# A two-model transformer kernel on one core: order of the work at block one's seams

## Chip, cores and metric

One NeuronCore of a Trainium2 chip. The metric is the device time of one launch in microseconds (us); the median of several runs counts. Engines are named as in the profile: PE is TensorE (PEld its weight loads), DVE is VectorE, ACT is ScalarE, POOL is GpSimd, SP is SyncE, which here issues every DMA. An "L" number is a line of the kernel before, unless the text says that it is one of the changed kernel.

## What is computed

256 tokens of width 1024 pass through two layers of a first block and then two layers of a second one. The change touches the first block, and the places where one layer follows another. Cut to that:

```python
for l in range(2):                                   # first block
    h = rms_norm(x, attn_norm_g[l])
    proj = h @ w_in[l]          # latents, GQA q/k/v, pool input, gate logits
    ...                         # three branches, each gated, summed in merged
    x = x + merged @ w_out[l]
    hf = rms_norm(x, ffn_norm_g[l])
    u = depthwise_conv(hf @ ffn_w_up[l], ...)        # 3 taps along the tokens
    u_gate, u_val = u[..., :2816], u[..., 2816:]
    x = x + (silu(u_gate) * u_val) @ ffn_w_down[l]
for i in range(2):                                   # second block
    h = x @ w_in_2[i]           # no norm ahead of it
    ...                         # two attentions, layer norm, 32 experts, layer norm
```

## The kernel before

**Parts.** Everything is float32, and the dense products are made of three passes over rounded parts. A weight chunk of up to 128 x 2048 lands by DMA in one of three `raw` slots (1 MB each). ACT rounds it to `w_hi` (L253, "hi" of the chunk), DVE subtracts to get `w_lo` (L258, "lo"), and `mm3` (L286) runs hi x hi, lo x hi and hi x lo on PE (L288 to L290). Activations are split in the same way: `one_hT_hi` by ACT (L373) and `one_hT_lo` by DVE (L381), each out of the PSUM tile that PE's transposes filled. `Stream` counts chunks: `hi_to` and `lo_to` split all chunks up to a name, `parts` makes PE wait for the lo part, and a raw slot may be loaded again once the lo part of the chunk in it is made.

**Lots.** PSUM is used as four lots of two banks (2 x 512 floats a partition). A hand-written list, `order` in `block_one`, says which tile uses which lot in which turn; `claim` waits until the last user of the lot is drained.

**Order.** Each engine has a program written out by hand (`sync`, `tensor`, `scalar`, `vector` of `block_one` and `block_two`); an engine runs its own in order and waits on semaphores. The 256 tokens are two tiles, t0 and t1, of 128.

**Start of a layer of block one.** DVE makes statistics of x (`first_stats`), ACT the root (`root_act_of`, L805), DVE scales (`rms_scale`, L837, into `one_tmp`), PE transposes eight 128 x 128 pieces (`transpose_tile`, L848), ACT and DVE split the result (`xTt0`, `xTt1`), and PE multiplies with `lat0` and `lat1` (`first_part`, 128x416), then `gkv` (128x256), `gq`, `uq`, `ukv`, `pool0` and `pool1`. In layer 0, tables for block two are loaded (`load_tables`, after `pool1` in SP's program), DVE makes angles of them (`rotation_angles`, L1918 on) and ACT their sines (`rotation_sines`, L1905).

**From attention to the FFN.** `out_part` adds the product with `w_out` in lots `wot0` and `wot1`; DVE adds it to x (`add_out`, `add_halves`), the second norm follows in the same way (`fTt0`, `fTt1`), and PE starts the FFN when both tiles are split.

**FFN.** Eleven steps of 256 hidden columns (`ffn_pe`). A step's up product `H` is 2 banks (G for the gate, U for the value) x 2 x 8 x 3 = 96 matmuls of 128x256: the weights are the stationary side and all 256 tokens the moving one. A profile row names the moving operand first, so `lot<-one_hT_hi,w_hi 128x256` is such a matmul. ACT and DVE do the convolution's taps, silu, product and its hi and lo parts (`h_lo`, L755), while PE does the next step's H; then comes the down product `D` (24 matmuls of 128x512), and DVE adds its tiles `Y` to x (L1744; the last ones by halves, `add_last`, L1449, inside the next layer's program).

**Between the layers of block two.** PE runs 36 transposes of the identity (`E.warm(pe, SEAM_TURNS)`, L2282) whose results nobody reads, then the transposes of x and `ik`, whose matmuls are 128x72.

Of the kernel before, what the change touches and what calls it, by code (L numbers as in the profile page):

```python
# [23 lines left out]
ALU = mybir.AluOpType  # L24
# [52 lines left out]
SEAM_TURNS = 36  # L77
# [560 lines left out]
def ffn_ends(steps):  # L638
    return {f"U{e}": f"H{e}" for e in range(steps)} | {f"D{e}": f"Y{e}t1" for e in range(steps)}
# [49 lines left out]
def ffn_pe(K, L, ST, pe, steps, xT, h):  # L689
# [12 lines left out]
    def down(e, i=None):  # L702
        pe.wait_ge(K.sig["h_lo"], K.sig.at("h_lo", later(e + 1, i, 2)))
        for t in range(T):
            lot = L.claim(pe, f"Y{e}t{t}", i, 2)
            w = [v[:, 0:CHUNK].rearrange("p (k c) -> p k c", k=T) for v in ST.parts(pe, f"D{e}", i)]
            for n in range(2):
                for k in range(T):
                    last = mm3(pe, K.ps[lot][:, n, :], [v[:, e % 2, k, t * P:(t + 1) * P] for v in h],
                               [v[:, k, n * 512:(n + 1) * 512] for v in w], k == 0, k == T - 1)  # L710
                if i is None and e == steps - 1 and n == 0:
                    last.then_inc(K.sig["last_half"], 1)
            last.then_inc(L.filled(f"Y{e}t{t}"), 1)

    hidden(0)

    def step(e, i):
        hidden(e + 1, i)
        down(e, i)

    ffn_walk(pe, steps, step)
    down(steps - 1)


def ffn_act(K, L, ST, act, steps, first, second, wait_full, h_hi, tail):
# [21 lines left out]
    tail()  # L747
    high(e, None)


def ffn_dve(K, L, ST, dve, steps, first, second, add, h, enter, leave, tail):
# [28 lines left out]
    e = steps - 1  # L780
    tail()
    for t in range(T):
        L.wait_filled(dve, f"Y{e - 1}t{t}")
        L.wait_before(dve, f"Y{e - 1}t{t}")
        add(e - 1, None, t).then_inc(L.drained(f"Y{e - 1}t{t}"), 1)
        if t == 0:
            low(e, None)
# [158 lines left out]
def block_one(K, M, layer, before=None, tables=None):  # L946
    nc, A, sig, st = K.nc, K.A, K.sig, K.stat
    names = ONE_CHUNKS + ffn_chunks(FF_STEPS)
    order = [("xTt0", 2), ("xTt1", 3), ("lat", 0), ("gkv", 2), ("gq", 3), ("cT", 1), ("q0", 2), ("q1", 0), ("kv0", 1),
# [12 lines left out]
    stage.L, stage.ST, stage.sig = L, ST, sig  # L962
# [54 lines left out]
    def sync(sp):  # L1017

        if before is None:
            for t in range(T):  # L1020
                sp.dma_start(K.x[:, t, :], A["x"][0][t * P:(t + 1) * P, :]).then_inc(sig[f"x_in{t}"], 16)
# [4 lines left out]
        for name in ONE_CHUNKS:  # L1026
# [24 lines left out]
    def tensor(pe):  # L1051
# [218 lines left out]
        for t in range(T):  # L1270
            L.wait_drained(pe, f"fTt{t}")
        ffn_pe(K, L, ST, pe, FF_STEPS, hT, (M.h_hi, M.h_lo))

    def scalar(act):
# [39 lines left out]
        ST.hi_to(act, "ukv")  # L1314
        take("gq", M.lat[:, :, C_GQ:C_GK], lambda ps: ps[:, :, :])
# [7 lines left out]
        if tables:  # L1323
            rotation_sines(sig, tables, act)
# [92 lines left out]
        def last_step():  # L1417
# [4 lines left out]
            for b in range(2):  # L1422
# [14 lines left out]
                lambda e, i: act.wait_ge(sig["h_full"], sig.at("h_full", later(e + 1, i, 2))), M.h_hi, last_step)  # L1437

    def add_last(dve, link, t, c):
# [16 lines left out]
    def vector(dve, link):  # L1456
# [8 lines left out]
        def first_stats(t):  # L1465

            if before is None:
                dve.wait_ge(sig[f"x_in{t}"], 16)
            for c in range(2):
                if before:  # L1470
                    before.add_last(dve, link, t, c)
                last = stats_of(K, dve, t, c)
            link(last)
# [2088 lines left out]
```

## Time and profile before

| | us |
|---|---|
| median of 3 runs (lowest, highest) | 1821.15 (1818.53, 1832.74) |
| the profiled execution: device time | 1821.87 |
| the profiled execution: span from first to last instruction | 1820.0 |
| PE busy in the span | 1632.6 (90%) |
| DVE busy | 1095.7 (60%) |
| ACT busy | 749.0 (41%) |
| mean granted TensorE clock, share of 2.4 GHz | 0.958 |

A timeline row gives start, length, engine, line, operation, output and inputs, how many instructions were merged, and in brackets how long the engine had been idle and what ended it. The granted clock of a stretch (PEclk) is 1.00 at 2.4 GHz and 0.50 at 1.2 GHz.

### The profile page before, as it was taken

How to read it: one execution, taken by the hardware profiler on the slowest of the kernel's cores; microseconds unless marked ns; L12 is line 12 of the kernel's file. 1: busy time of each engine (PE TensorE's matmuls, PEld its weight loads, DVE VectorE, ACT ScalarE, POOL GpSimd, SP SyncE). 2: the span in 40 equal slices, each digit the busy share in tenths (PEclk: the TensorE clock that was granted, in tenths of full speed). 3: DMA queues.
4: the chain of work that ended last, by engine and by line, in shares of the span. 5: the costliest groups of instructions: out<-in, count | busy, mean ns of one | idle time of the engine just before them, and what ended most of it. 6: DMA issues, size and time to landing. Idle time of an engine off the chain costs nothing.

```text
span 1820.0 us, 25937 instructions
## 1 busy us (share of the span) xinstructions
PE 1632.6 (90%) x10562; PEld 1288.5 (71%) x10562; DVE 1095.7 (60%) x1550; ACT 749.0 (41%) x976; POOL 0.2 (0%) x4
## 2 busy tenths in 40 slices
PE   6999989998999989999999898968789998897776
PEld 5777779997887779998887676434468776753433
DVE  5776768778786857878477673222265966512124
ACT  3556545554546635554456541101034655311111
POOL 0000000000000000000000000000000000000000
PEclk9999999998999999999999999889999999899988
DMA  6552536554552445554544398999956437799996
GB/s 205 182 185 93 174 119 206 184 196 140 184 190 101 145 145 198 172 184 146 193 166 135 122 413 331 412 418 412 409 162 208 140 115 286 313 414 417 412 416 244
DMA packets 174271, 422.54 MB, mean 232 GB/s; under 512 B 15984, under 2 KB 68568, under 8 KB 157528
## 3 DMA queue, kind: packets, MB, share of 16 engines
q1 hardware_dynamic: 174168, 421.07, 63.0%
q8 instruction: 76, 1.25, 0.3%
q14 instruction: 27, 0.22, 0.0%
HBM read 419.99 MB, written 1.05 MB: 231 GB/s over the span
## 4 chain that ended last, share of the span: by engine, by line
PE 60%; DVE 15%; DMA 15%; issue 4%; ACT 3%; SPq 3%; DVEq 0%; ACTq 0%
PE lot L288 15%; PE lot L290 14%; PE lot L289 14%; DVE w_lo L258 5%; PE lot L2218 4%; DMA raw<-w_exp_up 3%; SPq L2115 3%; DMA e_hi<-w_exp_down 3%; PE lot L2292 2%; ACT w_hi L253 2%; PE lot L2188 2%; DMA e_hi<-w_exp_up 1%; DMA raw<-w_out 1%; DMA two_e_sqT<-w_exp_up 1%; DMA e_lo<-w_exp_up 1%
## 5 line engine op out<-in xcount | busy, mean ns | idle before, releaser
L258 DVE TENSOR_TENSOR w_lo<-raw,w_hi 128x2048 fp32r<-128x2048 f32 (+4 forms) x196 | 436.1, 2230 | 127.4 <-ACT w_hi L253 126.7
L253 ACT ACTIVATE w_hi<-raw 128x2048 fp32r<-128x2048 f32 (+4 forms) x196 | 365.2, 1867 | 144.2 <-PE lot L290 129.6
L288 PE MATMUL lot<-one_hT_hi,w_hi 128*128 128x256 f32 x704 | 200.9, 285 | 5.1 <-DVE one_hT_lo L381 5.1
L289 PE MATMUL lot<-one_hT_lo,w_hi 128*128 128x256 f32 x704 | 200.7, 285 | 0.0
L290 PE MATMUL lot<-one_hT_hi,w_lo 128*128 128x256 f32 x704 | 200.6, 285 | 0.0
L288 PE MATMUL lot<-w_hi,two_hT_hi 128*128 128x512 f32 (+1 forms) x448 | 180.6, 403 | 9.7 <-DVE two_hT_lo L381 4.2
L290 PE MATMUL lot<-w_hi,two_hT_lo 128*128 128x512 f32 (+1 forms) x448 | 175.6, 392 | 0.0
L289 PE MATMUL lot<-w_lo,two_hT_hi 128*128 128x512 f32 (+1 forms) x448 | 175.5, 392 | 0.0
L288 PE MATMUL lot<-w_hi,one_hT_hi 128*128 128x512 f32 (+2 forms) x384 | 151.5, 395 | 15.6 <-DVE w_lo L258 6.7
L290 PE MATMUL lot<-w_hi,one_hT_lo 128*128 128x512 f32 (+2 forms) x384 | 147.2, 383 | 0.0
L289 PE MATMUL lot<-w_lo,one_hT_hi 128*128 128x512 f32 (+2 forms) x384 | 147.0, 383 | 0.0
L288 PEld LDWEIGHTS lot<-one_hT_hi,w_hi 128*128 128x128 f32 x704 | 136.7, 194 | 6.4 <-issue 5.7
L289 PEld LDWEIGHTS lot<-one_hT_lo,w_hi 128*128 128x128 f32 x704 | 136.7, 194 | 0.7
L290 PEld LDWEIGHTS lot<-one_hT_hi,w_lo 128*128 128x128 f32 x704 | 136.6, 194 | 0.0
L288 PEld LDWEIGHTS lot<-w_hi,two_hT_hi 128*128 128x128 f32 x448 | 87.9, 196 | 30.9 <-issue 7.4
L1734 DVE SCALAR_TENSOR_TENSOR one_conv<-lot,one_cols,one_conv 128x255 f32<-128x255 f32 x160 | 66.2, 476 | 58.2 <-ACT one_conv L1408 55.7
L290 PEld LDWEIGHTS lot<-w_hi,two_hT_lo 128*128 128x128 f32 x448 | 87.5, 195 | 17.7
L289 PEld LDWEIGHTS lot<-w_lo,two_hT_hi 128*128 128x128 f32 x448 | 87.8, 196 | 15.5
L288 PEld LDWEIGHTS lot<-w_hi,one_hT_hi 128*128 128x128 f32 x384 | 73.7, 192 | 34.0 <-issue 14.3
L2338 DVE COPY two_xw<-lot 128x512 f32<-128x512 f32 x16 | 11.1, 692 | 132.7 <-PE lot L2188 132.7
L2218 PE MATMUL lot<-raw,two_xw 128*32 128x256 f32 x448 | 82.1, 454 | 9.1 <-DMA e_hi<-w_exp_up 6.4
L2392 DVE TENSOR_TENSOR two_y_lo<-lot,two_y_hi 128x1024 fp32r<-128x1024 f32 x14 | 17.1, 1224 | 114.1 <-ACT two_y_hi L2359 114.1
(435 smaller groups left out, 3250.3 us busy)
## 6 DMA issues: line engine op xcount, KB each, us to landing
raw<-w_in SPq DMA_DIRECT2D x78, 1024.0 KB, 4.9
raw<-ffn_w_up SPq DMA_DIRECT2D x44, 1024.0 KB, 5.1
raw<-ffn_w_down SPq DMA_DIRECT2D x22, 1024.0 KB, 4.9
raw<-w_out SPq DMA_DIRECT2D x16, 1024.0 KB, 6.4
raw<-w_exp_gate SPq DMA_DIRECT2D x14, 1024.0 KB, 18.4
raw<-w_exp_up SPq DMA_DIRECT2D x14, 1024.0 KB, 20.6
two_e_gates<-w_exp_up SPq DMA_DIRECT2D x12, 1024.0 KB, 19.7
e_lo<-w_exp_up SPq DMA_DIRECT2D x10, 1024.0 KB, 22.1
```

Of the source, the lines that this page charges most:

```text
L253: act.activation(K.hi[:, r, 0:n], self.raw(name)[:, 0:n], ACT.Copy).then_inc(K.sig["hi_ready"], 1)
L258: dve.tensor_tensor(K.lo[:, r, 0:n], self.raw(name)[:, 0:n], K.hi[:, r, 0:n].bitcast(F32), ALU.subtract).then_inc(K.sig["lo_ready"], 1)
L288: pe.matmul(out, a[0], b[0], start=start, stop=False)
L289: pe.matmul(out, a[0], b[1], start=False, stop=False)
L290: return pe.matmul(out, a[1], b[0], start=False, stop=stop)
L1734: last = dve.scalar_tensor_tensor(dst, src, w, dst, ALU.mult, ALU.add)
L2115: sp.dma_start(dst.rearrange("p (k c) -> p k c", k=self.parts[name[0]]), self.source(name[0], expert)).then_inc(self.landed(name), 16)
L2188: last = pe.matmul(K.ps[1][:, lot - 2, kk * QE * CAP:(kk + 1) * QE * CAP], M.xg[:, t, k, :], M.rows01[:, t, :], start=t == 0, stop=t == T - 1)
L2218: last = pe.matmul(K.ps[0][j * CAP:(j + 1) * CAP, lot, half * D_E:(half + 1) * D_E], M.xw[:, k, rows], w[j][:, k, :], start=k == 0, stop=k ...
L2292: last = pe.matmul(K.ps[1][:, lot - 2, :], M.nT[:, k, t * P:(t + 1) * P], w[:, k % 4, :], start=k == 0, stop=k == KD - 1)
L2338: dve.tensor_copy(dst, src).then_inc(self.L.drained(f"X{q}.{j}"), 1)
L2392: dve.tensor_tensor(self.M.y_lo[:, s, :], flat(self.K.ps[2][:, :, :]), self.M.y_hi[:, s, :].bitcast(F32), ALU.subtract).then_inc(self.L.dr ...
```

## The change

1. **First FFN step by token tile.** The last quarter of `w_out` (`out_part(1, 1, 1)`) now runs ahead of the transposes of `fTt0`. The up product of step 0 is cut by token tile: G and U for t0, then for t1, 48 matmuls of 128x128 in each of four pieces, 192 in place of 96. The transposes of `fTt1` stand behind the first piece. DVE splits `G0` earlier, adds both halves before it makes the lo part of t0, and the statistics of the second half come behind that.
2. **Last two down products in one lot.** Steps 9 and 10 of the down product accumulate in the same PSUM lots; DVE's two additions of step 9 to x (128x1024 each) are gone. The H and Y lots of the last step and most lots at the layer's start are others.
3. **Order at a layer's start.** ACT takes the root of t0 and the hi part of t0 before it splits more weights; DVE makes the lo part of `lat0` and of t0 before the second half of t1's statistics. At the end of a layer ACT splits the next layer's first chunk before the hidden part's hi.
4. **Loads in layer 0.** x's second tile is loaded behind `lat0`; the tables behind `gq0`, not behind `pool1`; ACT makes the sines before it takes `gq` out of PSUM.
5. **Between the layers of block two** the 36 transposes of the identity are gone.

```diff
 def ffn_lots(steps):
     order = [("H0", 0)]
-    for e in range(1, steps):
+    for e in range(1, steps - 1):
         order += [(f"H{e}", e % 2), (f"Y{e - 1}t0", 2), (f"Y{e - 1}t1", 3)]
-    return order + [(f"Y{steps - 1}t0", (steps - 1) % 2), (f"Y{steps - 1}t1", steps % 2)]
+    e = steps - 1
+    return order + [(f"H{e}", e % 2), (f"Y{e}t0", 2), (f"Y{e}t1", 3)]
...
+    def down_two():
+        e = steps - 1
+        pe.wait_ge(K.sig["h_lo"], K.sig.at("h_lo", e))
+        for t in range(T):
+            lot = L.claim(pe, f"Y{e}t{t}")
+            for n in range(2):
+                last = part(e - 1, lot, t, n, stop=False)
+        ST.done(last, f"D{e - 1}")
+        pe.wait_ge(K.sig["h_lo"], K.sig.at("h_lo", e + 1))
+        for t in range(T):
+            lot = L.use[f"Y{e}t{t}"][0]
+            part(e, lot, t, 0, start=False).then_inc(K.sig["last_half"], 1)
+            part(e, lot, t, 1, start=False).then_inc(L.filled(f"Y{e}t{t}"), 1)
...
     tail()
+    if after:
+        after.ST.hi_to(act, after.first)
     high(e, None)
...
-    order = [("xTt0", 2), ("xTt1", 3), ("lat", 0), ("gkv", 2), ("gq", 3), ("cT", 1), ("q0", 2), ("q1", 0), ("kv0", 1),
+    order = [("xTt0", 1), ("xTt1", 0), ("lat", 2), ("gkv", 1), ("gq", 0), ("cT", 3), ("q0", 2), ("q1", 1), ("kv0", 0),
...
+            if before is None and name == "lat0":
+                sp.dma_start(K.x[:, 1, :], A["x"][0][P:S, :]).then_inc(sig["x_in1"], 16)
-            if tables and name == "pool1":
+            if tables and name == "gq0":
+                load_tables(nc, A, sig, tables, sp)
                 sp.dma_start(K.rope[:, :, :], A["c_rope"]).then_inc(sig["rope_in"], 16)
-                load_tables(nc, A, sig, tables, sp)
...
+        out_part(1, 1, 1).then_inc(L.filled("wot1"), 1)
         transpose_tile(K, L, pe, M.tmp, "fTt0", 0, sig, "n2_normed")
-        out_part(1, 1, 1).then_inc(L.filled("wot1"), 1)
+        def first_hidden(bank, t):
+            name = "GU"[bank] + "0"
+            w = [v[:, 0:CHUNK].rearrange("p (k c) -> p k c", k=KD) for v in ST.parts(pe, name)]
+            for f in range(2):
+                for k in range(KD):
+                    last = mm3(pe, K.ps[L.use["H0"][0]][:, bank, f * S + t * P:f * S + (t + 1) * P],
+                               [v[:, k, f * P:(f + 1) * P] for v in w], [v[:, k, t * P:(t + 1) * P] for v in hT],
+                               k == 0, k == KD - 1)
...
+        L.claim(pe, "H0")
+        L.wait_drained(pe, "fTt0")
+        first_hidden(0, 0)
         transpose_tile(K, L, pe, M.tmp, "fTt1", 1, sig, "n2_normed")
-        for t in range(T):
-            L.wait_drained(pe, f"fTt{t}")
+        first_hidden(1, 0)
+        L.wait_drained(pe, "fTt1")
+        first_hidden(0, 1)
+        first_hidden(1, 1)
...
-        ST.hi_to(act, "lat0")
-        root_act_of(K, act, "n1", 0)
+        if before:
+            ST.hi_to(act, "lat1")
+        root_act_of(K, act, "n1", 0)
+        ST.hi_to(act, "lat0")
+        tile_hi(0)
         ST.hi_to(act, "lat1")
         root_act_of(K, act, "n1", 1)
-        tile_hi(0)
         tile_hi(1)
...
-        first_stats(0)
+        first_stats(0, 0)
+        first_stats(0, 1)
         rms_var(K, dve, link, "n1", 0)
         rms_scale(K, dve, link, "n1", 0, M.tmp, M.gain)
-        first_stats(1)
+        ST.lo_to(dve, "lat0")
+        first_stats(1, 0)
+        tile_lo(0)
+        first_stats(1, 1)
         rms_var(K, dve, link, "n1", 1)
-        ST.lo_to(dve, "lat0")
-        tile_lo(0)
...
-        add_halves(1)
+        ST.lo_to(dve, "G0")
+        add_half(1, 0)
+        stats_of(K, dve, 1, 0)
+        add_half(1, 1)
+        low_tile(0)
+        link(stats_of(K, dve, 1, 1))
         rms_var(K, dve, link, "n2", 1)
         rms_scale(K, dve, link, "n2", 1, M.tmp, M.gain)
-        ST.lo_to(dve, "G0")
+        ST.lo_to(dve, "U0")
         low_tile(1)
...
-        if before:
-            E.warm(pe, SEAM_TURNS)
-        else:
+        if ahead:
             ahead.L.wait_drained(pe, f"Y{FF_STEPS - 1}t0")
```

How the rows of three places change. On PE, from attention to the FFN, the kernel before has behind the last quarter of `w_out` the transposes of `fTt1` (L848) and then step 0 with all 256 tokens:

```order
L290 MATMUL lot<-w_hi,one_hT_lo 128x512
L848 MATMUL lot<-ident,one_tmp 128x128 [waits n2_normed,drained1]
L848 MATMUL lot<-ident,one_tmp 128x128 x3
L848 MATMUL lot<-ident,one_tmp 128x128 [waits n2_normed]
L848 MATMUL lot<-ident,one_tmp 128x128 x3
L288 MATMUL lot<-one_hT_hi,w_hi 128x256 [waits drained0,lo_ready,drained1,drained2]
L289 MATMUL lot<-one_hT_lo,w_hi 128x256
L290 MATMUL lot<-one_hT_hi,w_lo 128x256
```

The changed kernel has there the transposes of `fTt0` (its line L861) and then step 0 for tile t0 alone:

```order
L289 MATMUL lot<-w_hi,one_hT_lo 128x512
L861 MATMUL lot<-ident,one_tmp 128x128 [waits n2_normed,drained2]
L861 MATMUL lot<-ident,one_tmp 128x128 x3
L861 MATMUL lot<-ident,one_tmp 128x128 [waits n2_normed]
L861 MATMUL lot<-ident,one_tmp 128x128 x3
L287 MATMUL lot<-one_hT_hi,w_hi 128x128 [waits lo_ready,drained2,drained0]
L288 MATMUL lot<-one_hT_lo,w_hi 128x128
L289 MATMUL lot<-one_hT_hi,w_lo 128x128
```

The wait for tile t1 (drained1) has moved behind the first two pieces, and the moving side has become 128 wide.

On DVE, from the end of the FFN of layer 0 to the start of layer 1, before (L1744 adds a tile of step 9, L1449 is `add_last`, L258 the lo part of `lat0`):

```order
L1768 TENSOR_TENSOR one_conv<-one_conv 128x512 [waits silu,drained0]
L1744 TENSOR_TENSOR x<-x,lot 128x1024 [waits drained2,filled2]
L755 TENSOR_TENSOR one_h_lo<-one_conv,one_h_hi 128x512 [waits h_hi]
L1744 TENSOR_TENSOR x<-x,lot 128x1024 [waits drained3,filled3]
L258 TENSOR_TENSOR w_lo<-raw,w_hi 128x1664 [waits hi_ready]
L1449 TENSOR_TENSOR x<-x,lot 128x512 [waits drained2,last_half]
```

And in the changed kernel:

```order
L1805 TENSOR_TENSOR one_conv<-one_conv 128x512 [waits silu,drained0]
L774 TENSOR_TENSOR one_h_lo<-one_conv,one_h_hi 128x512 [waits h_hi]
L257 TENSOR_TENSOR w_lo<-raw,w_hi 128x1664 [waits hi_ready]
L1484 TENSOR_TENSOR x<-x,lot 128x512 [waits drained2,last_half]
L831 BN_STATS stat<-x 128x6 [waits dve_chain]
```

The two additions between the hidden part and the last halves are gone.

On ACT, at the very start, before (L253 is the hi part of `lat0`, then `lat1`; L805 the roots; L373 the hi parts of t0 and t1):

```order
L253 ACTIVATE w_hi<-raw 128x1664 [waits landed1]
L805 ACTIVATE stat<-stat 128x1 [waits n1_var]
L253 ACTIVATE w_hi<-raw 128x1664 [waits landed2]
L805 ACTIVATE stat<-stat 128x1 [waits n1_var]
L373 ACTIVATE one_hT_hi<-lot 128x8x128 [waits filled2]
L373 ACTIVATE one_hT_hi<-lot 128x8x128 [waits filled3]
```

And in the changed kernel:

```order
L818 ACTIVATE stat<-stat 128x1 [waits n1_var]
L252 ACTIVATE w_hi<-raw 128x1664 [waits landed1]
L372 ACTIVATE one_hT_hi<-lot 128x8x128 [waits filled1]
L252 ACTIVATE w_hi<-raw 128x1664 [waits landed2]
L818 ACTIVATE stat<-stat 128x1 [waits n1_var]
L372 ACTIVATE one_hT_hi<-lot 128x8x128 [waits filled0]
```

The first root no longer stands behind the landing of `lat0`, and the hi part of t0 no longer behind `lat1`.

## Rows read from the trace of the kernel before

**Rows 1.** The page's part 1: busy time, share of the span and instructions of PE.

```profile
PE 1632.6 (90%) x10562; PEld 1288.5 (71%) x10562; DVE 1095.7 (60%) x1550; ACT 749.0 (41%) x976; POOL 0.2 (0%) x4
```

**Rows 2.** Timeline of the first 20 us; last row: DMA issues, median us to landing.

```profile
11.59 1.59 ACT L253 ACTIVATE w_hi<-raw 128x1664 fp32r<-128x1664 f32 x1 [5.40 <-DMA raw<-w_in]
...
14.40 1.94 PE L848 MATMUL lot<-ident,one_tmp 128*128 128x128 f32 x8 [14.40 <-DVE one_tmp L837]
...
16.71 1.88 DVE L258 TENSOR_TENSOR w_lo<-raw,w_hi 128x1664 fp32r<-128x1664 f32 x1
...
19.78 0.71 PE L288 MATMUL lot<-w_hi,one_hT_hi 128*128 128x416 f32 x1 [3.44 <-DVE one_hT_lo L381]
...
one_gain<-attn_norm_g SPq DMA_DIRECT2D x1, 512.0 KB, 7.3
```

**Rows 3.** Timeline of layer 0 around the tables of block two, 50 to 101 us.

```profile
50.42 1.90 ACT L253 ACTIVATE w_hi<-raw 128x2048 fp32r<-128x2048 f32 x1
...
55.72 0.29 DVE L1918 CAST two_tri_r<-two_tri 128x256 fp32r<-128x256 f32 x1 [8.69 <-DMA two_slots<-c_slots]
...
58.07 2.28 DVE L258 TENSOR_TENSOR w_lo<-raw,w_hi 128x2048 fp32r<-128x2048 f32 x1
58.13 1.28 ACT L1905 ACT_TABLE_LOAD   x1
...
60.50 0.47 PE L288 MATMUL lot<-w_hi,one_hT_hi 128*128 128x512 f32 x1 [4.11 <-DVE w_lo L258]
...
100.74 0.47 PE L288 MATMUL lot<-w_hi,one_hT_hi 128*128 128x512 f32 x1 [0.96 <-DVE w_lo L258]
```

**Rows 4.** Timeline of layer 0 from attention to the first FFN steps.

```profile
240.94 1.29 PE L848 MATMUL lot<-ident,one_tmp 128*128 128x128 f32 x8 [3.50 <-DVE one_tmp L837]
...
242.26 1.02 ACT L373 ACTIVATE one_hT_hi<-lot 128x1024 fp32r<-128x1024 f32 x1 [2.45 <-PE lot L848]
243.57 1.22 DVE L381 TENSOR_TENSOR one_hT_lo<-lot,one_hT_hi 128x1024 fp32r<-128x1024 f32 x1
...
244.89 0.55 PE L288 MATMUL lot<-one_hT_hi,w_hi 128*128 128x256 f32 x1 [2.66 <-DVE one_hT_lo L381]
...
271.39 0.50 PE L288 MATMUL lot<-w_hi,one_h_hi 128*128 128x512 f32 x1 [1.52 <-DVE one_h_lo L755]
```

**Rows 5.** Stretches, PE alone: length, busy time (matmuls), granted clock, DMA.

```profile
244.89:248.81 3.92, 3.92 (x18) 0.50 0.87 285
250.00:260.00 10.00, 10.00 (x86) 1.00 0.57 205
859.80:864.20 4.40, 4.40 (x23) 0.50 0.83 183
864.20:870.00 5.80, 5.80 (x17) 0.50 1.04 387
```

**Rows 6.** PE at the start of block two: the two pieces of 128x72.

```profile
859.41 0.27 PE L288 MATMUL lot<-w_hi,two_hT_hi 128*128 128x72 f32 x1 [1.51 <-DVE two_hT_lo L381]
...
860.34 0.41 PE L288 MATMUL lot<-w_hi,two_hT_hi 128*128 128x72 f32 x1
...
863.97 0.41 PE L290 MATMUL lot<-w_hi,two_hT_lo 128*128 128x72 f32 x1
...
870.31 0.28 PE L288 MATMUL lot<-w_hi,two_hT_hi 128*128 128x72 f32 x1
...
872.21 0.28 PE L290 MATMUL lot<-w_hi,two_hT_lo 128*128 128x72 f32 x1
```

**Rows 7.** PE from the FFN of layer 0 to layer 1.

```profile
438.55 1.23 PE L848 MATMUL lot<-ident,one_tmp 128*128 128x128 f32 x8 [2.74 <-DVE one_tmp L837]
...
444.90 0.69 PE L288 MATMUL lot<-w_hi,one_hT_hi 128*128 128x416 f32 x1 [5.12 <-issue]
```

**Rows 8.** PE between the layers of block two.

```profile
1332.32 3.22 PE L2282 MATMUL lot<-ident 128*128 128x128 f32 x28 [2.18 <-issue]
...
1339.05 0.27 PE L288 MATMUL lot<-w_hi,two_hT_hi 128*128 128x72 f32 x1 [2.64 <-DVE two_hT_lo L381]
```

More of the change, by code:

```diff
@@ L705, in down, with part, ffn_act @@
             lot = L.claim(pe, f"Y{e}t{t}", i, 2)
-            w = [v[:, 0:CHUNK].rearrange("p (k c) -> p k c", k=T) for v in ST.parts(pe, f"D{e}", i)]
             for n in range(2):
[L708 to L712, printed above, removed]
-            last.then_inc(L.filled(f"Y{e}t{t}"), 1)
-    hidden(0)
+                last = part(e, lot, t, n, i)
+            last.then_inc(L.filled(f"Y{e}t{t}"), 1)
+    def part(e, lot, t, n, i=None, start=True, stop=True):
+        w = [v[:, 0:CHUNK].rearrange("p (k c) -> p k c", k=T) for v in ST.parts(pe, f"D{e}", i)]
+        for k in range(T):
+            last = mm3(pe, K.ps[lot][:, n, :], [v[:, e % 2, k, t * P:(t + 1) * P] for v in h],
+                       [v[:, k, n * 512:(n + 1) * 512] for v in w], start and k == 0, stop and k == T - 1)
+        return last
+    def down_two():
[11 more added lines that the diff above has]
+            part(e, lot, t, 1, start=False).then_inc(L.filled(f"Y{e}t{t}"), 1)
     def step(e, i):
         hidden(e + 1, i)
-        down(e, i)
+        if i is None and e == steps - 2:
+            down_two()
+        else:
+            down(e, i)
     ffn_walk(pe, steps, step)
-    down(steps - 1)
-def ffn_act(K, L, ST, act, steps, first, second, wait_full, h_hi, tail):
+def ffn_act(K, L, ST, act, steps, first, second, wait_full, h_hi, tail, after):
     def high(e, i):
@@ L779, in ffn_dve @@
     ffn_walk(dve, steps, step, enter, leave)
-    e = steps - 1
     tail()
-    for t in range(T):
[L783 to L787, printed above, removed]
+    low(steps - 1, None)
 ONE_CHUNKS = ["lat0", "lat1", "gkv", "gq0", "gq1", "uq", "ukv", "pool0", "pool1", "g4a", "g4b", "window",
@@ L961, in block_one @@
     stage = Layer()
-    stage.L, stage.ST, stage.sig = L, ST, sig
+    stage.L, stage.ST, stage.sig, stage.first, stage.after = L, ST, sig, "lat0", None
     K.h = M.conv[:, 1, :, :]
@@ L1019, in sync @@
         if before is None:
-            for t in range(T):
-                sp.dma_start(K.x[:, t, :], A["x"][0][t * P:(t + 1) * P, :]).then_inc(sig[f"x_in{t}"], 16)
+            sp.dma_start(K.x[:, 0, :], A["x"][0][0:P, :]).then_inc(sig["x_in0"], 16)
             sp.dma_start(K.ident[:, :], A["c_ident"]).then_inc(sig["ident_in"], 16)
@@ L1314, in scalar @@
         ST.hi_to(act, "ukv")
+        if tables:
+            rotation_sines(sig, tables, act)
         take("gq", M.lat[:, :, C_GQ:C_GK], lambda ps: ps[:, :, :])
@@ L1322, in scalar @@
             take(f"kv{t}", M.kv[:, t, :])
-        if tables:
-            rotation_sines(sig, tables, act)
         ST.hi_to(act, "g4a")
@@ L1436, in scalar @@
         ffn_act(K, L, ST, act, FF_STEPS, middle_tap, silu,
-                lambda e, i: act.wait_ge(sig["h_full"], sig.at("h_full", later(e + 1, i, 2))), M.h_hi, last_step)
+                lambda e, i: act.wait_ge(sig["h_full"], sig.at("h_full", later(e + 1, i, 2))), M.h_hi, last_step, stage.after)
     def add_last(dve, link, t, c):
@@ L1463, in mul, with first_stats @@
             return dve.tensor_tensor(out, a, b, ALU.mult)
-        def first_stats(t):
-            if before is None:
+        def first_stats(t, c):
+            if before:
+                before.add_last(dve, link, t, c)
+            elif c == 0:
                 dve.wait_ge(sig[f"x_in{t}"], 16)
-            for c in range(2):
-                if before:
-                    before.add_last(dve, link, t, c)
-                last = stats_of(K, dve, t, c)
-            link(last)
+            last = stats_of(K, dve, t, c)
+            if c:
+                link(last)
         def tile_lo(t):
@@ L2504, in block_two @@
     stage = Layer()
-    stage.L, stage.ST, stage.after = L, ST, None
+    stage.L, stage.ST, stage.first, stage.after = L, ST, "ik", None
     x_sig, x_normed = (before.sig, "n2_normed") if before else (None, None)
@@ L2654, in first_part @@
                     last.then_inc(L.filled(name), 1)
-        if before:
-            E.warm(pe, SEAM_TURNS)
-        else:
+        if ahead:
             ahead.L.wait_drained(pe, f"Y{FF_STEPS - 1}t0")
@@ L3509, in build @@
         two1 = block_two(K.layer(ONE_COUNTS, ONE_COUNTS, TWO_COUNTS), two, 1, before=two0, out=out)
-        two0.after = two1
+        one0.after, one1.after, two0.after = one1, two0, two1
         with nc.Block() as block:
```

38 lines of the change are left out of this document (18 added, 20 removed).

## The prediction

> **What bounds the kernel now.** I read the page's part 1 first: PE is busy 90% of the span [rows 1], so the time is PE's work plus the stretches in which PE waits. Then the list of who waited for whom, for PE alone, and the timeline at each wait that the change touches. The reader is to see three things. At the start PE's first transposes come at 14.40 and its first product at 19.78; ACT stood behind the landing of `lat0` until 11.59 [rows 2]. At 60.50 PE waits 4.11 for a lo part that DVE makes late, because DVE had waited 8.69 for block two's tables [rows 3]. From attention to the FFN PE waits 3.50 and 2.66 [rows 4], and between the layers 2.74 and 5.12 [rows 7]. Last I read the granted clock of stretches and the pace of narrow matmuls [rows 5, 6], since the change makes 192 of them in each layer. There the sign is decided. All sums stand against the profiled execution: span 1820.0, device time 1821.87, which is 0.7 above the median of 1821.15; I carry the difference over to the median.
>
> **Start and tables (layer 0).** With the root first, DVE scales t0 as soon as the gain is there (issued at about 2.1, 7.3 to landing [rows 2]), so PE's transposes are done before `lat0` is split. From its landing the chain is hi 1.59, lo 1.88 [rows 2], half a tile's statistics (an estimate of 0.6, half of the 1.22 that DVE takes for a tile [rows 4]), lo of t0 1.22, handovers 0.2: 5.5. With `lat0` landing at 11.59 as before PE starts at 17.1; with x's 0.5 MB no longer ahead of it, it lands up to 1.35 earlier (0.52 MB at the 387 GB/s of [rows 5]) and PE starts at 15.8. So 2.7 to 4.0 are won; I take 4, since x1 is really moved behind `lat0`. The tables then are issued behind `gq0` and have landed long before DVE asks. ACT's hi part of `pool0` ended at 52.32 [rows 3]; it now ends at 52.3 - 4 + 1.7 (sine table load 1.28 and two short instructions, now ahead of it) = 50.0, and DVE's lo part starts there instead of at 58.07. DVE is busy without a gap from there until PE waits for it again at 100.74 [rows 3], so the whole stage moves by 8.1, and no more: PE alone could gain 4 + 4.1 + what the low clock behind that wait costs. Nothing gained if something else holds `pool0`: -4. Term: **-8.1** (-4 to -9).
>
> **FFN of layer 0 to layer 1.** Two additions to x are gone from DVE, and the lo part of t0 no longer waits for all of t1's statistics. PE's products end at 438.55 - 2.74 = 435.81 [rows 7]. The last half of t0 is added and scaled some 2 earlier, transposes at 436.4, hi and lo (1.02, 1.22 [rows 4]) behind them, DVE free for the lo part at 438.9: PE's product starts at 440.1, not at 444.90. What is late next is the lo part of `lat1`, made behind the scaling of t1: PE waits some 1 for it, of which 0.6 is a loss. The 48 matmuls of steps 9 and 10 stay 48, and the chunk split early on ACT fits where ACT idled. Term: **-4.2** (-1 to -5.5). From block one to block two PE is held by its own last product and a bare hi and lo chain: 0.
>
> **First FFN step by token tile (twice).** Before, PE's work ahead of the FFN ends at 240.94 - 3.50 = 237.44, then come wait, transposes, wait, and step 0 starts at 244.89 [rows 4]. After, the same work ends with the transposes of t0, and only their hi and lo (1.02 + 1.22, handovers 0.4) is bare: start at 240.1, 4.8 earlier. Against this stands the price of width. No row has a 128-wide product of rounded parts. From above: 256 wide takes 10.00/86 = 0.116 at 2.4 GHz and 3.92/18 = 0.218 at 1.2 GHz [rows 5]. From below: 72 wide takes (872.21 - 870.31)/17 = 0.112 and (863.97 - 860.34)/17 = 0.2135 [rows 6]. Narrowing to 72 saved 4% and nothing: something that doesn't shrink with the width, as loading the weights, sets the pace. So a 128-wide one costs 0.112 to 0.116, and 0.2135 to 0.218 at the lower clock; 96 become 192 at nearly the same price. At 2.4 GHz: 48 x 0.112 = 5.4, transposes 1.0, 144 x 0.112 = 16.1, so H0 is full at 262.6. Before it was full at 269.87 (= 271.39 - 1.52) less 96 x 0.117 = 258.6. That is +4.0, carried on, because the wait of 1.52 for the hidden part hangs on H0's end.
>
> The clock is the larger part. At the start of block two PE had the same pattern: wide matmuls, transposes, a wait of 1.51, narrow matmuls. The clock fell to 1.2 GHz within half a us of the first narrow one and stayed there through all the rest of them and 5.8 of wide ones [rows 5, 6]; elsewhere wide matmuls alone had it back after 3.92 [rows 5]. Here the wait is longer (2.3 to 2.7) and what follows is narrow again, now for more than 20 us. I expect the clock to fall about 1 us into the piece in four of five cases (how the wait lies in time decides), and to stay down until step 1's 256-wide ones have run for 4 to 6. Then: 0.9 at the high clock (8 matmuls), 184 x 0.2135 = 39.3, transposes 2.0: H0 full at 282.3. Step 1 takes 96 x 0.117 = 11.2 plus 2.5 for the low clock: 296.0, and by then the hidden part is ready, so no wait. Against 271.39: +24.6 a layer. Term for both layers: **+49.2** (+8 if the clock holds in both).
>
> The Trainium skill (TensorE: Matmul & The Clock Gate, Part 1) says that sustained matmuls release the throttle, and shows it on a stream of 128-wide ones. By that rule the clock would be back within the first quarter of the step and the total come to about 1824; rows 5 and 6 speak against it, as PE was busy without a gap there and the clock did not come back.
>
> **Between the layers of block two.** The 28 last identity transposes end at 1335.54 and hold back the real ones [rows 8]. Without them these start 2 earlier, the product about 0.9 earlier, since DVE is then the later one. But PE is idle where it was busy, the clock falls sooner and the 24 matmuls of 128x72 cost 24 x (0.2135 - 0.112) = 2.4 more, and a little behind them. Term: **+2** (-1 to +4).
>
> **Sum.** -8.1 - 4.2 + 0 + 49.2 + 2 = +38.9: 1821.87 becomes 1860.8, and the median 1821.15 becomes **1860**. The likeliest case has its own range of 1852 to 1867.
>
> **Rivals.**
> (a) *The low clock strikes in one layer only.* One wait lies so that the clock holds, and a step at the high clock keeps it. For it: the clock held across 1.52 at 271.39 [rows 4]. Then -8.1 - 4.2 + 2 + 24.6 + 4.0 = +18.3: 1839.
> (b) *The clock holds or comes back during the step, in both layers: not slower.* Its place is the four narrow pieces, its price 4.0 a layer, or 6 to 7 if it falls and returns after some 5 us. -8.1 - 4.2 + 2 + 8.0 = -2.3, up to +3: 1819 to 1824. It decides if 128-wide matmuls count as work for the clock where 72-wide ones didn't; between 72 and 256 no row tells. Against it: rows 5 and 6.
> (c) *The narrow matmuls are cheap.* If cost goes with width, 128 wide takes 0.058, the 192 take 11.2, the token split wins 6.3 a layer, and the clock has no reason to stay down: -8.1 - 4.2 + 2 - 12.6 = -22.9: 1798. Against it: 0.112 for 72 wide [rows 6]. The Trainium skill (same page, Back-to-back issue gap) gives 81 ns for a stream of 128-wide matmuls with their weight loads; by that the total would be about 1807, and the same rows contradict it for these operands.
> (d) *The change doesn't do what it says* at the start, because the gain or the first chunk lands later than I think: PE starts at 19 as before and the first term is -4. That only adds 4 to each case.
>
> **How the numbers follow.** Likeliest case 0.52, (a) 0.22, (b) 0.18, (c) 0.08. The range leaves out (c) and a little at the top: 1820 to 1867. Faster or slower by over 1% (18 us; about what a measurement of this kernel can tell from no change): faster only in (c), 0.06; slower in the likeliest case and in half of (a), 0.64; the rest, 0.30, within 1%.
>
> **What would show it.** Right: step 0's 192 matmuls take some 40 us with a granted clock of 0.50 over most of them, and spacings near 0.21; the page's mean clock falls below 0.958 by some 0.02. DVE waits under 1 for the tables, PE's first product comes at 16 to 17, and PE's wait at 60 is gone. Layer 1's first product comes 4 to 5 sooner behind the last down product. Wrong: narrow products spaced by 0.112 at a clock of 1.00 (then b), by 0.06 to 0.08 (then c), or a first product still near 19 (then d).

## The result, and the profile after

The changed kernel takes **1838.08 us** (median of 20 runs, 1823.22 to 1853.58) where the kernel before, beside it, took 1825.42 (20 runs, 1818.53 to 1834.82). The medians are 12.7 apart, a ratio of 1.0069. The ratio computed beside the runs is 1.0043, 95% interval 1.0025 to 1.0061; it leaves out the four runs at 1853 as disturbed, although here they are a state of the kernel's own, as shown below. The forecast was 1860, 38.9 more than the kernel before: the sign was right, the size three times too large.

The 20 times are three heaps: 5 runs from 1823.2 to 1824.8, 11 from 1835.4 to 1839.9, 4 from 1852.5 to 1853.6. The mean granted clock goes with them: 0.956 to 0.959, 0.944 to 0.950, 0.938 to 0.941. The profiled execution is one of the top heap: span 1851.7, device time 1853.48, clock 0.938. So what its trace shows in detail happened in 4 of the 20 runs.

The page's part 1 of the kernel after, which answers to [rows 1]:

```profile
PE 1683.6 (91%) x10718; PEld 1342.5 (73%) x10718; DVE 1091.9 (59%) x1546; ACT 748.7 (40%) x976; POOL 0.2 (0%) x4
```

The timeline of the kernel after (start, duration, engine, line, operation, in brackets the idle time before it), first the start and the tables, which answer to [rows 2, 3]:

```profile
8.61 1.94 PE L861 MATMUL lot<-ident,one_tmp 128*128 128x128 f32 x8 [8.61 <-DVE one_tmp L850]
...
10.09 1.59 ACT L252 ACTIVATE w_hi<-raw 128x1664 fp32r<-128x1664 f32 x1 [3.61 <-DMA raw<-w_in]
...
15.38 0.72 PE L287 MATMUL lot<-w_hi,one_hT_hi 128*128 128x416 f32 x1 [4.83 <-DVE one_hT_lo L380]
...
46.21 1.90 ACT L252 ACTIVATE w_hi<-raw 128x2048 fp32r<-128x2048 f32 x1
...
48.15 2.29 DVE L257 TENSOR_TENSOR w_lo<-raw,w_hi 128x2048 fp32r<-128x2048 f32 x1 [3.10 <-ACT w_hi L252]
...
90.85 0.47 PE L287 MATMUL lot<-w_hi,one_hT_hi 128*128 128x512 f32 x1 [0.94 <-DVE w_lo L257]
```

PE's first product comes 4.4 earlier (15.38, was 19.78), the wait of 4.11 near 60 is gone, and the wait that stood at 100.74 stands at 90.85: 9.9 are won. Then the seams of block one, which answer to [rows 4, 7]:

```profile
226.52 1.03 PE L861 MATMUL lot<-ident,one_tmp 128*128 128x128 f32 x8
...
230.04 0.30 PE L287 MATMUL lot<-one_hT_hi,w_hi 128*128 128x128 f32 x1 [2.49 <-issue]
...
239.47 1.93 PE L861 MATMUL lot<-ident,one_tmp 128*128 128x128 f32 x8
...
285.05 0.50 PE L287 MATMUL lot<-w_hi,one_h_hi 128*128 128x512 f32 x1
...
449.97 1.23 PE L861 MATMUL lot<-ident,one_tmp 128*128 128x128 f32 x8 [0.79 <-DVE one_tmp L850]
...
453.62 0.68 PE L287 MATMUL lot<-w_hi,one_hT_hi 128*128 128x416 f32 x1 [2.42 <-issue]
```

One wait of 2.49 is left of two at the first seam. But the first product with the hidden part comes at 285.05, 55.0 after the first of step 0; before it was 26.5. From there to layer 1's first product (453.62) it takes 168.57 and took 173.51: 4.9 won.

Last the same step in stretches, PE alone (start and end, length, busy time and matmuls, granted clock, DMA share, GB/s), layer 0:

```profile
230.04:239.60 9.56, 9.56 (x49) 0.55 0.40 128
239.60:241.40 1.80, 1.80 (x11) 0.50 1.04 402
241.40:271.80 30.40, 30.40 (x144) 0.50 0.14 46
271.80:275.30 3.50, 3.50 (x17) 0.50 0.00 0
275.30:285.00 9.70, 9.70 (x82) 1.00 0.34 110
```

PE has no gap in it. The clock falls 1.0 after the first product and stands at its lower level (1.2 GHz) through all that follow; the last 144 narrow ones take 30.4, 0.211 each. It comes back 3.5 after the first product of 256 columns. Layer 1 of this execution:

```profile
669.07:671.30 2.23, 2.23 (x20) 1.00 0.22 72
671.30:712.20 40.90, 40.90 (x194) 0.50 0.22 77
712.20:722.00 9.80, 9.80 (x83) 1.00 0.34 109
```

The balance of the profiled pair, stage by stage. Each layer has a wait of 0.96 or 0.97 behind attention that ends at 191.55 and 630.59 (201.44 and 621.55 before). The time to the first of them is 9.9 shorter. From it to the first product with the hidden part it is +23.5 in layer 0 and +22.4 in layer 1 (630.59 to 722.91, 92.3 long, was 69.9); -4.9 between the layers; -0.1 in the rest of block one and +0.6 in block two. Sum +31.6; the spans differ by 31.7 (1851.7 and 1820.0). The profiled execution of before is also 3.6 under the median of its 20 runs, as that of after is 15 over its own.

### The profile page after: what moved, and what is told of

Same layout as the page of the kernel before. It is cut to its first block, busy times and chain, and to the rows that moved or that the text cites. A ratio compares the mean times of both kernels' runs of the same rounds, so it can differ in the third digit from the quotient of the medians.

```text
span 1851.7 us, 26241 instructions
## 1 busy us (share of the span) xinstructions
PE 1683.6 (91%) x10718; PEld 1342.5 (73%) x10718; DVE 1091.9 (59%) x1546; ACT 748.7 (40%) x976; POOL 0.2 (0%) x4
## 4 chain that ended last, share of the span: by engine, by line
PE 62%; DVE 14%; DMA 13%; SPq 4%; issue 3%; ACT 3%; DVEq 0%; ACTq 0%
PE lot L287 16%; PE lot L289 16%; PE lot L288 16%; DVE w_lo L257 4%; SPq L2152 4%; DMA e_hi<-w_exp_down 4%; DMA raw<-w_exp_up 3%; PE lot L2255 3%; DMA raw<-w_exp_gate 2%; ACT w_hi L252 2%; PE lot L2282 1%; PE lot L2329 1%; PE lot L2225 1%; DMA raw<-w_out 1%; DMA e_hi<-w_exp_up 1%
## 5 line engine op out<-in xcount | busy, mean ns | idle before, releaser
L287 PE MATMUL lot<-one_hT_hi,w_hi 128*128 128x256 f32 (+1 forms) x768 | 234.4, 305 | 5.0 <-issue 5.0
L289 PE MATMUL lot<-one_hT_hi,w_lo 128*128 128x256 f32 (+1 forms) x768 | 234.2, 305 | 0.0
L288 PE MATMUL lot<-one_hT_lo,w_hi 128*128 128x256 f32 (+1 forms) x768 | 234.1, 305 | 0.0
L287 PEld LDWEIGHTS lot<-one_hT_hi,w_hi 128*128 128x128 f32 x768 | 165.4, 215 | 6.1 <-issue 5.4
L288 PEld LDWEIGHTS lot<-one_hT_lo,w_hi 128*128 128x128 f32 x768 | 165.4, 215 | 0.7
L289 PEld LDWEIGHTS lot<-one_hT_hi,w_lo 128*128 128x128 f32 x768 | 165.4, 215 | 0.0
L288 PEld LDWEIGHTS lot<-w_lo,two_hT_hi 128*128 128x128 f32 x448 | 87.5, 195 | 15.3
L2255 PE MATMUL lot<-raw,two_xw 128*32 128x256 f32 x448 | 77.8, 430 | 8.9 <-DMA e_hi<-w_exp_up 5.0
```

The costliest lines, as they stand in the source:

```text
L287: pe.matmul(out, a[0], b[0], start=start, stop=False)
L288: pe.matmul(out, a[0], b[1], start=False, stop=False)
L289: return pe.matmul(out, a[1], b[0], start=False, stop=stop)
L2255: last = pe.matmul(K.ps[0][j * CAP:(j + 1) * CAP, lot, half * D_E:(half + 1) * D_E], M.xw[:, k, rows], w[j][:, k, :], start=k == 0, stop=k ...
```

## The experiments

The theory (C): in each layer the clock falls behind PE's wait of 2.49 and then either comes back early in the narrow step or not at all in it (the layer is "stuck"). The three heaps are executions with no layer, one layer and both layers stuck. The rivals are in the expectations. The kernel before was run again beside each group of experiments; ratios are to those runs.

**1. The step whole again.** The seam from attention to FFN as before, on PE and DVE; the rest of the change stays.

```diff
+    hidden(0)
...
-        out_part(1, 1, 1).then_inc(L.filled("wot1"), 1)
         transpose_tile(K, L, pe, M.tmp, "fTt0", 0, sig, "n2_normed")
+        out_part(1, 1, 1).then_inc(L.filled("wot1"), 1)
...
         transpose_tile(K, L, pe, M.tmp, "fTt1", 1, sig, "n2_normed")
-        first_hidden(1, 0)
-        L.wait_drained(pe, "fTt1")
-        first_hidden(0, 1)
-        first_hidden(1, 1)
+        for t in range(T):
+            L.wait_drained(pe, f"fTt{t}")
```

> The changed kernel with the first FFN step whole again (96 products of 256 columns, the seam from attention to FFN on PE and DVE as before); all other parts stay. Theory C (the clock, layer by layer: the runs of the changed kernel lie near 1823.5, 1838 and 1853, 14.8 apart, because the narrow step runs at 1.2 GHz in none, one or both layers; the other parts gained what the profile shows, 9.9 at the start and tables, 4.7 between the layers): before less 9.9 and 4.7 = 1811 (1808 to 1814), one level only, spread as in before. Rival W (the other parts gave back later what they won early, and the narrow step is what costs nothing at its best): about 1823, the lowest level of the changed kernel, since only the levels above it belong to the split.

Measured 1808.95 (5 runs, 1805.92 to 1811.40), ratio 0.9902 (0.9876 to 0.9928), one heap. The other parts kept what they won (the profiled spans are 15.9 apart, 1804.1 and 1820.0); W falls. Without its first part the change is 1% faster than before.

**2. The split alone.** The kernel before with the token split and its order on DVE, that is, with the same lines the other way round.

> The kernel before with the split of the first FFN step by token tile alone (with its DVE order at that seam). Theory C: the lowest level is the changed kernel's lowest plus the 14.6 that the other parts won, 1838, and further levels stand 14.8 and 29.6 above, 1853 and 1868; mean granted clock lower by about 0.009 for each level. Rival W: levels at 1825, 1840 and 1855.

Measured 1858.98 (5 runs, 1857.61 to 1860.47), ratio 1.0176 (1.0150 to 1.0202). All five lie in one heap, between two of those expected. The trace says which: layer 0 had the clock back, layer 1 did not.

```profile
240.11:241.80 1.69, 1.69 (x15) 1.00 0.38 118
241.80:252.10 10.30, 10.30 (x51) 0.50 0.55 196
252.10:268.00 15.90, 15.90 (x144) 1.00 0.03 7
668.11:712.90 44.79, 44.79 (x212) 0.50 0.21 75
```

So it is the heap of one stuck layer. I had put it at 1853 and missed by 6, because I took the gain of the other parts from one pair of profiles. The heap stands 31.3 above the runs of before beside it (1827.66). In this trace the two layers are 9.0 and 24.1 longer than before (201.62 to 280.52 and 629.59 to 723.62), 33.1 together. Why all five runs fell into one heap is open.

**3. The wait filled.** Ten products of 512 columns where PE stood idle:

```diff
+        def fill(turns):
+            w = ST.parts(pe, "G0")[0]
+            for _ in range(turns):
+                pe.matmul(K.ps[3][:, 1, :], w[:, 0:P], w[:, 0:512], start=True, stop=True)
+
+        L.wait_drained(pe, "wot0")
+        fill(10)
         L.claim(pe, "H0")
         L.wait_drained(pe, "fTt0")
```

> The changed kernel with 10 products of 512 columns (of G0's hi part, into a PSUM lot that is free and is overwritten later) in PE's wait between the transposes of t0 and the first narrow product, so that PE does not stand idle there. The output is the same. Theory C (the clock falls because of the wait, and 128-wide products neither take a high clock away nor give it back): granted clock 1.00 through the whole narrow step in both layers, spacing 0.112, each layer saves the low stretches even of the lowest level: 1812 to 1820, one level only, mean clock 0.960 or more. Rival N (the narrow products themselves let the clock fall, wait or no wait): step 0 at 0.50 again and levels at 1823, 1838, 1853, more often the upper ones than before.

Measured 1813.98 (6 runs, 1811.40 to 1814.73), ratio 0.9923 (0.9900 to 0.9946). One heap, 24 under the changed kernel's median. The stretches of PE, first layer 0 (filler; narrow step and the transposes in it), then both layers from the same wait in attention to the hidden part:

```profile
227.16:229.68 2.52, 2.52 (x13) 1.00 0.96 321
229.89:252.60 22.71, 22.71 (x203) 1.00 0.28 100
...
191.37:265.42 74.05, 72.30 (x475) 1.00 0.43 145
610.76:684.81 74.05, 72.30 (x474) 1.00 0.43 145
```

203 matmuls in 22.71 are 0.112 each, at a clock of 1.00 throughout. N falls: narrow products do not take a high clock away. And 74.05 less the 69.95 of before (201.44 to 271.39 [rows 4]) is +4.1: this is the price of a split layer at the high clock, with the shorter wait in it. Before's own step is not free of the low clock (0.50 up to 248.81 [rows 5]), so it is not yet the price of width alone; experiment 8 gives that.

**4. The changed kernel once more.**

> The changed kernel once more, for other executions of it. Theory C: times fall into the levels 1823.5, 1838 and 1853 with mean granted clocks near 0.957, 0.948 and 0.939 and nothing between; if the profiled execution is of one of the lower two, at least one layer's step 0 takes 26 to 31 us instead of 41.8, with the granted clock back at 1.00 after the first part of it. Rival D (the levels come from block two, whose transfers fall differently): step 0 takes 41.8 in both layers whatever the level, and the difference stands behind 890.

Measured 1838.43 (12 runs, 1823.20 to 1839.26): 2 runs at 1823, 10 from 1835.5 to 1839.3. The profiled execution (1838.69) is of the middle heap. Its layers, PE in stretches, and three rows of its timeline:

```profile
229.52:229.80 0.28, 0.28 (x3) 0.92 1.06 377
229.80:271.30 41.50, 41.50 (x198) 0.50 0.23 78
668.50:670.10 1.60, 1.60 (x15) 0.99 0.31 100
670.10:680.30 10.20, 10.20 (x51) 0.50 0.54 189
680.30:696.00 15.70, 15.70 (x142) 1.00 0.03 12
```

```profile
677.34 1.93 PE L861 MATMUL lot<-ident,one_tmp 128*128 128x128 f32 x8
...
695.69 0.33 PE L287 MATMUL lot<-one_hT_hi,w_hi 128*128 128x256 f32 x1
...
708.90 0.50 PE L287 MATMUL lot<-w_hi,one_h_hi 128*128 128x512 f32 x1 [1.48 <-DVE one_h_lo L774]
```

Layer 0 is stuck, in layer 1 the clock returned 1.0 after the eight plain float32 transposes of t1, and the step took 27.2 (668.50 to step 1's first product at 695.69) instead of 41.8. From the wait behind attention (630.00) to the hidden part layer 1 is 78.90 long, +9.0 against before's 69.89: the 4.1 of experiment 3 and 4.9 for the low stretch of 10.2. D falls. In the profile of after, the wait of layer 1 had ended at 669.07 instead of 668.50, the clock fell 1.2 later, the transposes stood at 677.33, and there it did not return.

The middle and the top heap are so read from traces. The lowest was never profiled: that it is two layers like this one is inferred. Its 1823 to 1825 fit, 9.6 above experiment 3, where the clock never falls, against 2 x 4.9.

**5. The wait filled with narrow products**, 21 of 128x128 for the ten wide ones:

```diff
-        fill(10)
+        fill(21)
...
+                pe.matmul(K.ps[3][:, 1, 0:P], w[:, 0:P], w[:, 0:P], start=True, stop=True)
```

> The changed kernel with PE's wait in the seam filled by 21 products of 128x128 (G0's hi part, into a free PSUM lot) in place of the 10 of 512 columns. The output is the same. Theory F (it is enough that PE is not idle: narrow products hold a high clock): as with the wide filler, no low clock in the seam, 1812 to 1816, one level. Rival G (narrow products hold the clock only behind something wide; here wait and narrow step are one long narrow stretch, and the clock falls in it): levels at 1823, 1838 or 1853 again.

Measured 1813.92 (6 runs, 1809.58 to 1819.56), ratio 0.9925 (0.9902 to 0.9948), and the clock at 1.00 from 190.55 to 264.53. F holds and G falls: with the idle time gone the clock stays, and narrow products are enough to fill it.

**6. Wide products inside the step**, the wait left open:

```diff
         first_hidden(0, 0)
+        L.wait_drained(pe, "wot0")
+        w = ST.parts(pe, "G0")[0]
+        for _ in range(8):
+            pe.matmul(K.ps[3][:, 1, :], w[:, 0:P], w[:, 0:512], start=True, stop=True)
         transpose_tile(K, L, pe, M.tmp, "fTt1", 1, sig, "n2_normed")
```

> The changed kernel with 8 products of 128x512 (G0's hi part, into a free PSUM lot) between the first narrow piece and the transposes of t1; the wait ahead of the step is left as it is. The output is the same. Theory R (once low, only something denser than narrow products brings the clock back; in some executions the transposes of t1 do it): with the wide ones beside them the clock returns there in every layer, low for about 10 to 14 us of each step: one level, 1823.5 plus 1.9 to 3.6 for the 8 products in each layer, 1827 to 1831. Rival S (whether the low clock stays is settled at the wait, and nothing in the step changes it): levels at 1827, 1842 and 1857 with the upper ones in three of four executions.

Measured 1829.61 (12 runs, 1824.65 to 1835.32), ratio 1.0005 (0.9988 to 1.0022). The upper heaps are gone in all 12 runs. Layer 0 of its profile, PE in stretches and two rows of its timeline; layer 1 reads alike (0.50 from 658.4 to 668.7):

```profile
229.94:231.80 1.86, 1.85 (x17) 0.99 0.32 106
231.80:242.00 10.20, 10.20 (x42) 0.50 0.56 198
242.00:258.00 16.00, 16.00 (x145) 1.00 0.02 6
...
238.58 3.64 PE L1303 MATMUL lot<-w_hi 128*128 128x512 f32 x8
242.05 1.04 PE L861 MATMUL lot<-ident,one_tmp 128*128 128x128 f32 x8
```

The clock falls as before and comes back 3.4 after the first wide product (4.2 in layer 1), in layer 0 before the transposes begin; the narrow ones behind them keep it. S falls.

**7. The tables in their old place**, on the kernel of experiment 1:

```diff
-            if tables and name == "gq0":
+            if tables and name == "pool1":
...
-        if tables:
-            rotation_sines(sig, tables, act)
         take("gq", M.lat[:, :, C_GQ:C_GK], lambda ps: ps[:, :, :])
```

> The first FFN step whole and all other parts of the change kept, but the tables loaded behind pool1 and the sines made behind kv1 as in the kernel before. Theory T (the tables' place removes a wait of its own): PE waits 4 to 5 again near 56 with a low clock behind it, and 5 to 6 of the 10 that the start and tables won are lost: 1814 to 1815. Rival U (most of the 10 comes from the root and the parts being in another order; DVE's wait is hidden by what was won ahead of it): 1809 to 1811.

Measured 1812.46 (6 runs, 1810.88 to 1814.91), ratio 0.9918 (0.9898 to 0.9938), 3.5 over experiment 1 and between what T and U expected. PE's timeline has the wait back:

```profile
14.43 0.71 PE L287 MATMUL lot<-w_hi,one_hT_hi 128*128 128x416 f32 x1 [4.64 <-DVE one_hT_lo L380]
...
55.48 0.76 PE L287 MATMUL lot<-w_hi,one_hT_hi 128*128 128x512 f32 x1 [4.61 <-DVE w_lo L257]
...
196.43 0.50 PE L287 MATMUL lot<-w_hi,one_mT_hi 128*128 128x512 f32 x1 [0.97 <-DVE one_mT_lo L512]
```

196.43 stands between 201.44 (before) and 191.08 (experiment 1): the other order and x's load are worth 5.0, the tables' place 5.3. T holds in the trace (the spans, 1809.3 and 1804.1, are 5.2 apart); by the medians, which were not measured beside each other, it is 3.5.

**8. The step whole, both waits filled**: what the experiments point to.

```diff
+                pe.matmul(K.ps[3][:, 1, :], K.ident[:, :], M.tmp[:, 0, 0:512], start=True, stop=True)
...
+        fill(3)
         transpose_tile(K, L, pe, M.tmp, "fTt1", 1, sig, "n2_normed")
+        fill(2)
```

> The first FFN step whole, all other parts of the change kept, and PE's two waits of that seam filled: 3 plain float32 products of 128x512 (identity times the normalised tile, into a free PSUM lot) ahead of the transposes of t1, 2 behind them. The output is the same. Theory C: the low clock of 6.8 us behind those waits goes in both layers; of it the transposes (1.69 to 1.94 instead of 1.03) and some 18 wide products (0.218 instead of 0.117) come back, 2 to 2.5 a layer: 1804.5 (1803 to 1806) against 1809 without the filler. Rival H (the products of the filler end late and push the transposes): 1809 to 1812.

> The step whole with both waits of its seam filled once more, beside the kernel with the identity transposes. Both theories: 1800 to 1804, and no low clock in the stretch from 190 to 420 us.

Measured 1801.71 (5 runs) and again 1800.44 (6 runs), ratios 0.9856 (0.9834 to 0.9878) and 0.9867 (0.9843 to 0.9891): the fastest kernel of this study, faster than the kernel before and the changed one. It beat what C expected (1803 to 1806); H falls. PE at the seam of layer 0:

```profile
192.11 0.50 PE L287 MATMUL lot<-w_hi,one_mT_hi 128*128 128x512 f32 x1 [0.97 <-DVE one_mT_lo L512]
...
235.59 0.36 PE L287 MATMUL lot<-one_hT_hi,w_hi 128*128 128x256 f32 x1 [1.00 <-DVE one_hT_lo L380]
...
260.39 0.50 PE L287 MATMUL lot<-w_hi,one_h_hi 128*128 128x512 f32 x1 [1.53 <-DVE one_h_lo L776]
```

From the wait behind attention to the hidden part it takes 68.28 in each layer, at a clock of 1.00, against 69.81 and 70.77 in experiment 1, so 4.0 are explained; the spans differ by 4.2 (1799.9 and 1804.1). That the medians differ by 7 to 8 is not explained.

This kernel and that of experiment 3 differ at the seam in the split and its order, and both are at the high clock there throughout. There step 0 begins 38.52 after the wait and lasts 35.53 to the hidden part; here it begins after 43.48 and lasts 24.80. So the split buys 5.0 and costs 10.7: 5.8 lost a layer. The 4.1 of experiment 3 is smaller only because before's step itself starts at the low clock.

**9. The identity transposes**, back on the kernel of experiment 8; then gone from the kernel before; then back on the kernel of experiment 1.

```diff
-        if ahead:
+        if before:
+            E.warm(pe, SEAM_TURNS)
+        else:
             ahead.L.wait_drained(pe, f"Y{FF_STEPS - 1}t0")
```

> The step whole with both waits filled (1801.7 above), and the 36 transposes of the identity between the layers of block two back in their place; it is to be compared with the same kernel without them, run beside it. Theory P (the prediction's term): with them 2 us faster, because the clock falls later behind the wait and the narrow products there run faster. Rival Q (the traces of before and after: the seam itself is 0.7 shorter without them and the part behind it 0.7 longer): no difference, within 1 us.

> The kernel before with one part of the change alone: the 36 transposes of the identity between the layers of block two are gone. Theory P (the prediction's term): +2, 1827 to 1829 against some 1826. Rival V (seen in the last pair: with them the seam took 13.70 from the last product to the first of the next layer, without them 10.90, because in that execution the 36 ran at the low clock and held back the real transposes): the seam is 0.7 to 2.8 shorter, 1819 to 1825.

> The first FFN step whole, all other parts of the change kept except that the 36 transposes of the identity are back. Theory P: 1807. Rival V: 1810 to 1812, with 11.6 to 13.7 from the last product of block two's first layer to the first of its second, against 10.9. If the 7 us of the last pair were theirs, 1816; if they were of the place at which the executions come to block two, nothing of the kind shows here.

Measured 1808.04 (6 runs) against 1800.44 without them beside it; 1823.49 (12 runs, ratio to before 0.9984, 0.9964 to 1.0004) without them against 1824.51 with them beside it; and 1809.97 (12 runs, 1806.12 to 1819.38) with them against 1808.95 without, not beside it. By the ratios to before (0.9927 and 0.9902) the last pair is 4.6 apart, but their intervals overlap. So the removal is worth something between nothing and the 7.6 of the first pair, and in no pair does it cost 2: P falls. In the first pair's trace most of the 36 ran at the lower clock, and they ended late:

```profile
1313.03 6.75 PE L2310 MATMUL lot<-ident 128*128 128x128 f32 x36 [2.28 <-issue]
...
1323.29 0.27 PE L288 MATMUL lot<-w_hi,two_hT_hi 128*128 128x72 f32 x1 [2.65 <-DVE two_hT_lo L381]
```

The traces of the other kernels say when it matters. From the first product of the last group in front of the seam to the first product of 512 columns behind both of its narrow pieces it takes 23.8 to 24.5 in the traces without the 36 (after, experiment 4, both of experiment 8, the kernel before without them), and with them 23.8 (before), 25.9 (the first pair) and 29.5 (experiment 1's kernel, in the slowest of its 12 runs, where all 36 ran at 0.50). So they cost nothing in the trace in which the clock was high under them, and 2 to 5.7 in the two in which it was low.

## Why the prediction was right or wrong

- **Start and tables, -8.1: right, a little small.** PE's first product came at 15.38 (forecast 15.8), `pool0`'s hi part ended at 48.11 (forecast 50.0), and DVE's stretch behind it carried this to 100.74 - 90.85 = 9.9, just outside of the -4 to -9 given. Experiment 7 splits it in about equal halves. Rival (d) did not happen.
- **Layer 0 to layer 1, -4.2: right.** 4.9, with waits of 0.79 and 2.42 left.
- **A split layer at the high clock, +4.0: right.** 4.1, at a spacing of 0.112 (experiment 3). Rival (c) fell: 128-wide products of these rounded parts cost what 72-wide ones do. With it fell the 1807 that was worked out from the 81 ns of the Trainium skill (TensorE: Matmul & The Clock Gate, Back-to-back issue gap): the trace has 112 ns for these operands.
- **A layer stuck at the low clock, +24.6: right for the layer.** 23.5 and 22.4 in the profile after, 24.1 in experiment 2; H0 was full 41.8 after its first product (42.2 in the working), and step 1 had the clock back after 3.5. The signs named for the likeliest case all stand in the profile after, the mean clock of 0.938 too; but that execution has both layers stuck, which was the rarest case.
- **The step that failed:** "I expect the clock to fall about 1 us into the piece in four of five cases [...] and to stay down". The fall was right: it came in every layer profiled of the kernels with the split and the open wait, 0.3 to 2.2 in. Staying down was wrong. By the heaps it stayed down in 29 of 64 layers (32 runs of the changed kernel: 7 with none, 21 with one, 4 with both), and in the others it returned after some 10 us, and such a layer cost +9.0 (experiment 4) in place of the 24.6 that I had put for both. I took [rows 5, 6] for the whole pattern. Their 5.80 at 0.50 is also not all of wide ones, as I read it: 12 products of 512 columns end after 5.3, and the clock came back among the narrow ones behind them. What brings it back in one execution and not in the other is not shown. In both layers that returned without help (experiments 2 and 4) the low stretch ended 10.2 to 10.3 after it began, soon behind the eight transposes of t1; but the same transposes stand in the stuck layers, so they do not suffice, and the fall came 1.6 and 1.7 in where it returned and 0.3, 0.4, 1.0 and 2.2 in where it stayed. Experiment 6 shows only that eight products of 512 columns in that place end the low stretch every time. With what was measured, the mean price of a layer is 0.45 x 23 + 0.55 x 9 = 15.3, not 24.6; twice that, less 9.9, 4.9 and an estimated 1 for the seam in block two, is +15, and the medians moved by 12.7.
- **Rival (a)** with one layer was put at 1839 and 0.22. It was the likeliest case: 1835 to 1840 in 21 of 32 runs. It hit partly by luck. Its layer that holds was priced at 4.0, not 9.0, but the terms outside of the step summed to -10.3 where the runs gave some -15.8, which about makes up for it. And its 1839 was +18.3 on a median of 1821.15 from 3 runs, where 20 runs give 1825.42 and the heap lies some 13 above that. **Rival (b)** (1819 to 1824, or -2 to +3) was the lowest heap, 2 under before; both were given too little, 0.22 and 0.18, against 0.52 for the case that came in 4 of 32 runs.
- **The Trainium skill** (TensorE: Matmul & The Clock Gate, Part 1) says that sustained matmuls release the throttle. The traces bear it out for products of 256 columns (3.5 in the profile after) and of 512 (3.4 in experiment 6), and contradict it for 128-wide ones of rounded parts: 30.4 without a gap did not bring the clock back.
- **Between the layers of block two, +2: wrong, small.** The price of the narrow products behind the wait is there and about cancels the earlier start (23.8 and 23.8 in the profiled pair). What I left out is that the 36 transposes can run at the low clock themselves and hold back the real ones (25.9 and 29.5 in experiment 9).

## What to carry to other kernels

A split that halves the width of products whose pace does not depend on the width buys a shorter wait with twice the matmuls: here 5.0 bought for 10.7, a loss even at the high clock. If the split stretch stands behind a wait, price it at both clocks, and look at the list of single run times for heaps before reading a median. Where PE must wait 2 to 4 us in front of a long stretch, try to fill the wait with products into a free PSUM lot: here it did not delay the step (38.52 after the wait behind attention with the filler, 38.49 without), the low clock was gone from the step in every trace with a filler, and the times made one heap.

## What the runs showed of the hardware that was not expected

The same instructions had two stable paces. 128-wide products kept a granted clock of 1.00 (203 matmuls in 22.71, experiment 3) and in the profile after did not regain it from 0.50 (144 in 30.40). A shift of 0.6 in the end of the wait (668.50 against 669.07) went with the one or the other, and such differences made steps of some 14.7 us in the total. What in the position decides was not tried. Nor is it settled why kernels whose profiles differ by 4 in block one have medians that differ by 7 to 8 (experiment 8): block two has some twenty low stretches of its own, and their places differ from one execution to another.
